# Gate products of a PEER feed-forward kernel moved from one float32 product to two products on split operands

## The reference, cut to what matters

```python
v1, i1 = lax.top_k(s1, 16); v2, i2 = lax.top_k(s2, 16)
cand = v1[..., :, None] + v2[..., None, :]           # 256 a head
top_s, top_pos = lax.top_k(cand, 16)
ids = take_along_axis(i1[..., :, None] * 128 + i2[..., None, :], top_pos)
g = softmax(top_s)
act = einsum('thkd,td->thk', u[ids], x)
y = einsum('thk,thkd->td', g * gelu(act), v[ids])    # sum over heads and k
```

## Time and profile before

| | us |
|---|---|
| median of 3 runs | 3306.89 (3303.33 to 3310.65) |
| profiled execution, its time | 3303.13 |
| profiled execution, its span | 3301.3 |
| PE busy | 3255.4 (99%) |
| PE weight loads busy | 3032.6 (92%) |
| DVE busy | 2609.4 (79%) |
| ACT busy | 1556.3 (47%) |
| POOL busy | 1100.7 (33%) |

### The profile page before, as it was taken

The page is one execution under the profiler, slowest core; times in us unless marked ns, Lnnn a source line. Parts: engine busy times, 40 slices in busy tenths (PEclk is TensorE's granted clock), DMA queues, the critical chain, the costliest instruction groups (busy, mean ns, idle before and its releaser), DMA issues. The chain is left out here.

```text
span 3301.3 us, 55810 instructions
## 1 busy us (share of the span) xinstructions
PE 3255.4 (99%) x19734; PEld 3032.6 (92%) x19734; DVE 2609.4 (79%) x4992; ACT 1556.3 (47%) x2368; POOL 1100.7 (33%) x711
## 2 busy tenths in 40 slices
PE   8999999999999999999999999999999999999998
PEld 7767888999999999999987678889999999999998
DVE  6555448999997899999865644399999978999997
ACT  5554332467774333333355543334677733333333
POOL 1000003423335665555300000134333355555552
PEclk9999999999999999999999999999999999999999
DMA  4113322479999999999721133225899999999996
GB/s 146 63 52 114 141 108 79 173 289 382 377 382 390 419 402 411 408 410 411 293 90 64 52 122 141 101 77 190 313 377 381 380 408 411 405 407 406 407 406 250
DMA packets 230935, 894.83 MB, mean 271 GB/s; under 512 B 22784, under 2 KB 67984, under 8 KB 182912
## 3 DMA queue, kind: packets, MB, share of 16 engines
q1 hardware_dynamic: 116944, 465.34, 36.9%
q0 software_dynamic: 93008, 337.91, 26.1%
q10 hardware_dynamic: 20832, 89.74, 6.7%
HBM read 801.42 MB, written 91.49 MB: 270 GB/s over the span
## 5 line engine op out<-in xcount | busy, mean ns | idle before, releaser
L843 DVE TENSOR_TENSOR lo<-raw,hi 128x2048 fp32r<-128x2048 f32 (+1 forms) x320 | 729.2, 2279 | 287.9 <-ACT hi L508 277.9
L1332 PE MATMUL bank<-xT_hi,hi 128*128 128x352 f32 (+1 forms) x2688 | 927.2, 345 | 1.9 <-DVE xT_lo L893 1.7
L1333 PE MATMUL bank<-xT_lo,hi 128*128 128x352 f32 (+1 forms) x2688 | 910.7, 339 | 0.0
L1334 PE MATMUL bank<-xT_hi,lo 128*128 128x352 f32 (+1 forms) x2688 | 910.6, 339 | 0.0
L508 ACT ACTIVATE hi<-raw 128x2048 fp32r<-128x2048 f32 (+1 forms) x338 | 644.3, 1906 | 370.4 <-PE bank L1334 328.2
L1332 PE MATMUL bank<-w_hi,hi 128*128 128x352 f32 x2048 | 661.1, 323 | 0.7 <-DVE w_lo L1250 0.7
L1334 PE MATMUL bank<-w_hi,lo 128*128 128x352 f32 x2048 | 659.2, 322 | 0.0
L1333 PE MATMUL bank<-w_lo,hi 128*128 128x352 f32 x2048 | 657.2, 321 | 0.0
L1332 PEld LDWEIGHTS bank<-xT_hi,hi 128*128 128x128 f32 x2688 | 506.4, 188 | 31.6 <-issue 5.3
L497 POOL DMA_INDIRECT rows<-in_v_rows,ids x256 | 415.0, 1621 | 346.7 <-DVE h L1222 274.7
L1334 PEld LDWEIGHTS bank<-xT_hi,lo 128*128 128x128 f32 x2688 | 505.7, 188 | 25.4
(11 more groups left out here) (227 smaller groups left out, 4268.4 us busy)
## 6 DMA issues: line engine op xcount, KB each, us to landing
raw<-in_stream SPq DMA_DIRECT2D x352, 1024.0 KB
gate_d<-gate_s ACTq DMA_DIRECT2D x22, 2048.0 KB
act_d<-act_s ACTq DMA_DIRECT2D x120, 352.0 KB
act_in<-act_d SPq DMA_DIRECT2D x120, 352.0 KB
gate_in<-gate_d SPq DMA_DIRECT2D x96, 384.0 KB
gate_in<-gate_d SPq DMA_DIRECT2D x32, 256.0 KB
rows<-in_u_rows,ids POOLq DMA_INDIRECT x256
rows<-in_v_rows,ids POOLq DMA_INDIRECT x256
```

Source lines behind the costliest of these rows:

```text
L843: dve.tensor_tensor(lo[s][:, 0:n], raw[s][:, 0:n], hi[s][:, 0:n].bitcast(F32), ALU.subtract).then_inc(lo_done, 1)
L1332: pe.matmul(dst, a_[0], b_[0], start=first, stop=False)
L1333: pe.matmul(dst, a_[0], b_[1], start=False, stop=False)
L1334: return pe.matmul(dst, a_[1], b_[0], start=False, stop=last)
```

## The change

1. **Gate products.** For each token two fp32r products take the place of the float32 product. Both have `oh2` (iota == idx2) as the stationary operand; the moving ones are `oh1[..., 0]` and `oh1[..., 1]`, the one-hot of idx1 times the high and times the low half of the gate. DVE makes both with one `scalar_tensor_tensor` of 256 elements. The gates' low half is three small subtractions behind `idx_ev`.
2. **Second halves by POOL.** From chunk FIND_STEPS + 1 to 63 (`SHARED`) DVE subtracts columns 0 to 1023 of `lo`, and POOL then columns 1024 to 2047, in order with its row fetches. PE's half i = 0 waits for DVE's, i = 1 for POOL's.
3. **Rows from PSUM.** The input with which the rows of `u` are multiplied is copied by ACT into PSUM banks 2 and 3: `x_e` in gate step 0, `x_row` in gate step 10 (behind the 32nd row operation). DVE's row operations read it there. The `v` chunks' first use of bank 2 waits for the last row of `u`; the order of the banks changes for it.
4. **Lookup by ranks.** The compare and the predicated copy for a = 1 to 15 cover only ranks a to 15 of each 16, instead of all 16.
5. **Schedule.** FIND_STEPS is 12 instead of 14, so the gates begin two steps earlier and the tail has 22 steps; `LOW_HALF_AT` has 3 entries instead of 5; the gelu and the weighing of the 32 tokens move two steps forward in the gate stage.
6. Small buffers are packed or moved into the free columns of `xT_hi` and `xT_lo`; a zero operand of 512 columns becomes a broadcast of one.

```diff
-FIND_STEPS = 14
+FIND_STEPS = 12
-EXP_STEP, IDX_AT = 7, {13: (0, 1, 2)}
+EXP_STEP, IDX_AT = 7, {11: (0, 1, 2)}
-V_BLOCKS = (2, 3, 4, 5, 6, 7, 0, 1)
+V_BLOCKS = (4, 5, 6, 7, 2, 3, 0, 1)
-E_GELU, E_WEIGH = 12, 14
+E_GELU, E_WEIGH = 10, 12
-LOW_HALF_AT = (3, 5, 8, 10, 13)
+SHARED = range(FIND_STEPS + 1, C_U)
+def rows_by(st):
+    if st >= G_STEPS:
+        return ROWS_IN_G + (st + 1 - G_STEPS) * (U_ROW_OPS - ROWS_IN_G) // TAIL_STEPS
+    n = st * ROWS_IN_G // (G_STEPS - 1)
+    return min(n, E) if st <= E_GELU else n
+LOW_HALF_AT = (2, 5, 9)
...
 POOL
+                for n in range(NR):
+                    fetch(n)
+                n = NR
+                for c in SHARED:
+                    second_half(c)      # waits lo0_done, subtracts half of the chunk, lo_done
+                    while n < rows_by(c - SHARED.start) + NR:
+                        fetch(n)
+                        n += 1
...
 ACT
+                    if st == 0:
+                        act.wait_ge(e_link, 5 * l + 5)
+                        act.activation(x_in_ps, x_e, ACT.Copy).then_inc(x_ps_set, 1)
                     if st == E_GELU:
                         act.wait_ge(row_done, ROW_OPS * l + E)
+                        act.activation(x_in_ps, x_row[:], ACT.Copy).then_inc(x_ps_set, 1)
...
 DVE
-                        at[a] = looked(dve.tensor_scalar(chosen[a % 2], slot_f, float(a), None, ALU.is_equal))
+                        at[a] = looked(dve.tensor_scalar(by_rank(chosen[a % 2])[:, :, a:], by_rank(slot_f)[:, :, a:],
+                                                         float(a), None, ALU.is_equal))
...
+                for tt in range(NDT):
+                    low = dve.tensor_tensor(g_hl[:, tt, 1], ps[2 + tt][:, 2 * P:3 * P], g_hl[:, tt, 0].bitcast(F32), ALU.subtract)
...
-                            last = dve.tensor_scalar(o[:, r, 0], iota[:], idx1T[:, t], gT[:, t], ALU.is_equal, ALU.mult)
+                            last = dve.scalar_tensor_tensor(
+                                out=oh1[:, slot, r], in0=bc(iota[:], 1, 2), scalar=of_token(idx1T, q * G_TOK + r),
+                                in1=bc(g_hl[:, tt, :, t0 + r].bitcast(F32), 2, P), op0=ALU.is_equal, op1=ALU.mult)
...
-                    ahead(p, s)
+                    c = FIND_STEPS + st + 1
+                    if c in SHARED:
+                        dve.wait_ge(hi_done, 2 * (lp + P_U) + c + 1)
+                        half = slice(0, HALF)
+                        dve.tensor_tensor(lo[c % 2][:, half], raw[c % 2][:, half], hi[c % 2][:, half].bitcast(F32),
+                                          ALU.subtract).then_inc(lo0_done, 1)
+                    else:
+                        wait_alone(dve, lo_done, 2 * (lp + P_V) + CR, dve_passed)
+                        ahead(p, s)
...
 PE
                     for r in range(G_TOK):
-                        last = pe.matmul(ps[4 + slot][:, tile(r)], o[:, 1], o[:, 0], start=True, stop=True)
+                        for x in range(2):
+                            last = pe.matmul(ps[4 + slot][:, tile(r)], oh2[:, slot, r], oh1[:, slot, r, x],
+                                             start=x == 0, stop=x == 1)
...
+                        if first and d == 2:
+                            pe.wait_ge(row_done, ROW_OPS * l + U_ROW_OPS)
```

More of the change, by code:

```diff
@@ L223, in sem, with bank @@
             return ctx.enter_context(nc.semaphore(name))
-        ps = [ctx.enter_context(nc.psum_tensor(f"bank{i}", [P, T], F32)) for i in range(8)]
+        def bank(i, shape):
+            return ctx.enter_context(nc.psum_tensor(f"bank{i}", shape, F32))
+        ps = [bank(i, [P, T]) for i in range(2)]
+        x_ps_row = bank("2_3", [P, 2, T])
+        ps += [x_ps_row[:, i] for i in range(2)]
+        ps += [bank(i, [P, T]) for i in range(4, 8)]
+        x_in_ps = x_ps_row[:].rearrange("p b t -> p (b t)")
         h = sb("h", [P, NT, D])
@@ L244, in build @@
         pos_i, pos_f = sb("pos_i", [P, NT], I32), sb("pos_f", [P, NT])
-        eps, one = sb("eps", [P, 1]), sb("one", [P, 1])
-        zero_r = sb("zero_r", [P, T], F32R)
+        small = sb("small", [P, 3])
+        eps, one, zero = (small[:, i:i + 1] for i in range(3))
         ss, rms, rstd = sb("ss", [P, NT]), sb("rms", [P, NT]), sb("rstd", [P, NT])
-        mx, nmx = sb("mx", [P, NU]), sb("nmx", [P, NU])
-        den, esink, rden = sb("den", [P, NU]), sb("esink", [P, NU]), sb("rden", [P, NU])
+        stats = sb("stats", [P, P])
+        mx, nmx, den, esink, rden = (stats[:, i * NU:(i + 1) * NU] for i in range(5))
         to_line = sb("to_line", [P, 8])
@@ L284, in build @@
         ids = sb("ids", [P, P], U32)
[L285 removed]
+        act_row = stats
+        g_row, w_row = sb("g_row", [P, P]), sb("w_row", [P, P])
         ids_e = sb("ids_e", [P, E], U32)
@@ L302, in build @@
         gate_s = sb("gate_s", [P, 2, P, SLICE], to=table)
-        onehot = sb("onehot", [P, G_RING, G_TOK, 2, P], to=table)
+        oh2 = sb("oh2", [P, G_RING, G_TOK, P], F32R, table)
+        oh1 = sb("oh1", [P, G_RING, G_TOK, 2, P], F32R, table)
         rows = sb("rows", [P, NR + 1, D], to=table)
@@ L489, in _, with fetch @@
                 wait_alone(pool, ids_done, 2 * l + 2, pool_passed)
-                for n in range(ROW_OPS):
+                def fetch(n):
                     N, k = ROW_OPS * l + n, n % U_ROW_OPS
@@ L499, in _, with second_half @@
                                             ).then_inc(rows_in[N % NR], 16)
+                def second_half(c):
+                    s, half = c % 2, slice(HALF, CW)
+                    pool.wait_ge(lo0_done, LO0_PER_LAYER * l + len(HALVED) + c - FIND_STEPS)
+                    pool.tensor_tensor(lo[s][:, half], raw[s][:, half], hi[s][:, half].bitcast(F32),
+                                       ALU.subtract).then_inc(lo_done, 1)
+                for n in range(NR):
[6 more added lines that the diff above has]
+                        n += 1
+                while n < ROW_OPS:
+                    fetch(n)
+                    n += 1
         @block.scalar
@@ L1207, in row_op @@
                     dve.wait_ge(rows_in[N % NR], 16 * (N // NR + 1))
+                    if n in (0, E):
+                        dve.wait_ge(x_ps_set, 2 * l + (1 if n == 0 else 2))
                     if n < E:
-                        last = dve.tensor_tensor_reduce(row, row, x_e, 1.0, 0.0, ALU.mult, ALU.add, act_e[:, n:n + 1])
+                        last = dve.tensor_tensor_reduce(row, row, x_in_ps, 1.0, 0.0, ALU.mult, ALU.add, act_e[:, n:n + 1])
                     elif n < U_ROW_OPS:
-                        last = dve.tensor_tensor_reduce(row, row, x_row[:], 1.0, 0.0, ALU.mult, ALU.add, act_row[:, k])
+                        last = dve.tensor_tensor_reduce(row, row, x_in_ps, 1.0, 0.0, ALU.mult, ALU.add, act_row[:, k])
                     elif n < U_ROW_OPS + E:
@@ L1278, in _ @@
                         weigh_lo(0)
-                    while n < (st * ROWS_IN_G // (G_STEPS - 1) if st < G_STEPS else ROWS_IN_G + (st + 1 - G_STEPS) * (U_ROW_OPS - ROWS_IN_G) // TAIL_STEPS):
+                    while n < rows_by(st):
                         row_op(n)
@@ L1596, in _, with experts @@
                 q_steps(PH // 2 - 1, True)
-                def experts(j, s, i, first=0, end=NK, halved=None):
+                def experts(j, s, i, first=0, end=NK, halved=None, shared=False):
                     k = l * C_U + 2 * j + s
@@ L1602, in experts @@
                         if halved is not None and i == 0:
-                            pe.wait_ge(lo0_done, len(HALVED) * l + halved - 1)
-                        elif halved is not None or i == 0:
+                            pe.wait_ge(lo0_done, LO0_PER_LAYER * l + halved - 1)
+                        elif shared and i == 0:
+                            pe.wait_ge(lo0_done, LO0_PER_LAYER * l + len(HALVED) + 2 * j + s - FIND_STEPS)
+                        elif halved is not None or shared or i == 0:
                             take(lp + P_U + j, s)
@@ L1639, in g_step @@
                     for i in range(2):
-                        experts(j if it is None else j + it * (G_RING // 2), s, i)
+                        experts(j if it is None else j + it * (G_RING // 2), s, i, shared=st > 0)
                         for b in range(i, 2 * i + 1):
@@ L1655, in _ @@
                         for i in range(2):
-                            experts(j, s, i)
+                            experts(j, s, i, shared=True)
                 pe.wait_ge(g_ev, GROUPS * (l + 1) + G_RING)
```

40 lines of the change are left out of this document (24 added, 16 removed).

## The result

The changed kernel took 3315.65 us (median of 17 runs, 3312.53 to 3320.59), the kernel before 3307.73 beside it (3302.88 to 3313.87): ratio 1.0025, 95% interval 1.0019 to 1.0032. It is slower by 7.9 us (0.25%, 5.8 to 10.6 by the interval), where 3310 (+2.8 on the 3306.9 then known) was forecast.

A forecast was written before the change was run, and what follows sets the result against it. PE was taken as the bound, busy 3255.4 of 3301.3 us. All terms were 0 except gate step 0: 2 x 1.4 = +2.8 us, giving a median of 3310; likeliest range 3303 to 3314, 8 in 10 3289 to 3336.

The forecast's parts named there:

- PE's work for the gates, 0: Gate products: still 1408 passes at 0.112 us, each waiting for its weight load, so PE's work changes by 0.
- A: Rival, chance 0.17: gate passes set by their columns, loads hidden, 0.067 us each; DVE then bounds the gate stage; 3292 us.
- One-hot 0.388 us, VectorE's step 10.2: Gate step: new one-hots take DVE 0.388 us each, its step 10.2 us, hidden under PE's 10.35.
- POOL's halves 0 while the rows read PSUM: Shared halves: POOL's 2.44 us run beside DVE's row operations, which have one tensor in PSUM; cost 0.
- B: Rival, chance 0.2: one-hots run into POOL's late half, DVE bounds the gate step at 11.0 us; 3339 us.
- Two steps earlier, 0: End of find: ids and gates wanted 15.4 us sooner, DVE saves 16.5 us and ends as now relative to PE; 0.
- Gate step 0, +1.4 a layer: Gate step 0: ACT's copy of `x_e` waits for DVE and delays the gelu PE needs; +1.4 us a layer.
- Gate step 10, "3 us of room", 0: Gate step 10: ACT waits some 0.7 us for row 32, copies for 1.05; its gelu has 3 us of room; 0.
- First v chunk, 0: First `v` chunk: two rows (2.3 us) lie behind PE's starting weights; PE reaches bank 2 after 3.8 us; 0.
- if PE's step leaves 10.35 us: Gate stage: the stated sign that the prediction is wrong, PE's step leaving 10.35 us in either direction.
- the range of 8 in 10: Whole kernel: time forecast between 3289 and 3336 us, reaching into both rivals that have lines here.
- the likeliest case: Whole kernel: the forecast itself, 3310 us, with its own range 3303 to 3314 and chance 0.5.

The follow-up runs named there:

- e5: Changed kernel with gate products whose moving operand has 64 columns instead of 128 (half of each gate table left out); 3315.98 us, run once.
- e4: Changed kernel with gate products whose stationary operand has 64 columns instead of 128 (half of each gate table left out); 3303.45 us, run once.
- e2: Changed kernel with one gate product a token, on the high half alone; VectorE still makes both halves of the one-hots; 3302.01 us, ratio 0.9988.
- e6: Changed kernel with VectorE's row operations reading x from SBUF instead of PSUM, POOL's halves kept; 3447.82 us, ratio 1.0424.
- e7: Changed kernel with one float32 gate product a token again, on 128-element one-hots by tensor_scalar, gates rounded to the high half; 3306.30 us, ratio 1.0004.
- e1: Changed kernel with ACT's two copies into PSUM (gate steps 0 and 10) moved behind the first gelu of their step; 3308.61 us, ratio 1.0011.
- after 2: The changed kernel, unchanged, measured and profiled a second time; 3313.38 us, ratio 1.0025.
- before 2: The kernel before the change, profiled a second time; 3303.43 us.
- e3: Changed kernel with one gate product a token on the high half, VectorE making only that half, as 128-element one-hots by tensor_scalar; 3255.02 us, ratio 0.9841.

## Why the prediction was right, and where not

- *PE's work for the gates, 0.* Right: 0.111 us a pass before and after. A is refuted: e5 shows that fewer columns save nothing. Even with the pass at half price (e4, e2) VectorE would have kept all but 12 us, as A's sum assumed (15).
- *One-hot 0.388 us, VectorE's step 10.2.* Right: 0.396 and 9.9 with three rows; e2 and e4 show the length by itself, 10.21 and 10.24.
- *POOL's halves 0 while the rows read PSUM.* Right, and the cover is worth 134 us (e6). B's mechanism appeared in one step a layer, gate step 0 (7.62 us for twelve one-hots), where PE had no wait for it.
- *Two steps earlier, 0.* Right to 0.2 us: before, the transposes started 0.51 us behind the last product, 0.18 of it idle; now they start 0.24 behind it with no wait, and their step is shorter (8.74 us against 8.96, in one layer 8.85). The short compares kept their speed (0.43 us on the mean, 0.69 at full length), and the copies save 7.8 us a layer, where 8.1 was estimated.
- *Gate step 0, +1.4 a layer.* Right: 1.29, by the chain foretold. Only 0.96 of it is left with short one-hots (e7).
- *Gate step 10, "3 us of room", 0.* Wrong, the step that failed: +0.66 to 0.77 us a layer. I set the room from the start of ACT's gelu in an undisturbed step, and had ACT wait 0.7 us for row 32; it waited 2.98. VectorE's step had grown from 9.7 to 9.9 or 10.2 and used up its waits, so row 32 ended at 790.09, and PE wanted the gelu at 791.25: room of 1.16 us for a copy, a small gelu and the gelu itself, 1.6. e7, with short one-hots, brings the step to 10.35, and e1, with the copy moved, to 10.38.
- *First v chunk, 0.* It takes 7.66 to 7.76 us instead of 8.2: a gain of 0.5 us a layer that I had not seen. Before, PE waited 0.3 us there for the low half of the weighted operand (`w_lo`, written by VectorE); now it doesn't.
- *Missing in the sum.* The products between split gate passes are slower by 0.03 us a step, 0.9 us a layer, and so are those of the tail of layer 0, by 1.1 us in all. What the trace of before showed (10.353 in all steps) gave no hint of it.
- *The sign of being wrong, "if PE's step leaves 10.35 us".* It came: the steps are 10.37 to 10.41, and step 10 is 11.0 to 11.1.

The sum by stages, after 2 against before: copies 2 x 1.29 + 2 x 0.68 = 3.9; products of the gate steps 2 x 0.95 = 1.9; tail of layer 0 1.1; find 2 x 0.3 = 0.6 (a rhythm that varies in the kernel before too); first v chunk -0.9. Together 6.6 of the 7.9 measured; the rest is within the interval (+-2 us) and the v stage's scatter. Against before 2, whose find stage and tail were longer, the same stages give 5.2. The forecast's 2.8 had only the first half of the first term, 2 x 1.29. The time fell in the range of 8 in 10 (3289 to 3336), which reaches so far because of rivals A and B, and neither of them came; it lies just outside the own range of the likeliest case (3303 to 3314). So the main mechanisms were right, and that the range held owes something to luck.

Not settled: why products behind split passes fall into the uneven rhythm. That the passes' moving width matters is shown (e5, 64 columns, has 160 throughout and 10.36 us a step, though its VectorE works the same), not how. Two passes a token are not needed for it: in e2 and e3, with one fp32r pass, part of the groups behind the passes have 161.0 to 161.3 ns too (20 of 56 and 10 of 55 in layer 0), and so has the tail of layer 0 in e3 (170.18 us). With float32 passes one group of more than 450 has it, in the eight gate stages of four profiles.

## What to carry to other kernels

Exchanging a float32 product for two fp32r products saves nothing when each pass is shorter than its weight load; look at the distance of starts, not at the columns. Before a pass is taken out, read which engine has the next longest step: here 78 us of PE's work were worth 12, and 58 only when VectorE's step shrank too, with late transfers behind it. A copy that waits for a late producer belongs behind the urgent work of its engine's queue, and its room is counted from the producer's new end, not the old one.

## What the runs showed of the hardware

- Spacing of fp32r passes of 128 moving columns: 0.111 us with 128 stationary columns, 0.060 with 64; with 64 moving and 128 stationary 0.111.
- Products of 352 columns hold 158.9, 160.0 or 161.1 ns on the mean, for up to 62 of the 64 chunks of a v stage; which one varies between executions there. In the gate stages groups with 161 stand behind fp32r passes of 128 columns, and but for one nowhere else.
- A VectorE operation with both tensors in SBUF beside POOL's two-tensor operation: 1.21 us became 3.37, and POOL's 2.41 became 3.27; with one tensor in PSUM both kept their time (1.21 and 2.41).
- The granted clock was 1.00 in the gate stage as long as PE was busy; in e3, behind waits of PE of 1.6 to 3 us, it fell to the 1.2 GHz level for a while (0.69 on the mean of 757 to 762 us), with products of 352 columns 293 ns apart; behind waits of 0.4 and 0.5 us there it stayed at 1.00.
